# Row sums one group later, tiles scaled by ScalarE, the MLP's first chunk by 256 tokens, and roundings moved, in a two-block transformer kernel

## What is computed

```python
h_x = modulate(x, sh1, sc1)                 # LayerNorm, times 1 + scale, plus shift, from c
mix = (g_f * y_f + g_m * y_m + g_g * y_g) @ w_o      # Fourier, latent and grouped attention, gated
x = layer_norm(alpha * x + g1 * mix, ln1_g, ln1_b)
x = layer_norm(alpha * x + g2 * sq_relu_mlp(modulate(x, sh2, sc2)), ln2_g, ln2_b)
def sq_relu_mlp(h): return square(relu(h @ w1)) @ w2          # 1024 -> 4096 -> 1024
```

## Time and profile before

| what | us |
|---|---|
| three runs, median (lowest, highest) | 3475.98 (3465.0, 3476.44) |
| the profiled execution | 3469.96 |
| its span in the profile | 3468.2 |
| granted PE clock, mean | 0.95 |

### The profile page before, as it was taken

How to read it: one execution, slowest core, us unless ns; L and a number is a source line. 1 busy time by engine, 2 the same in 40 slices (tenths; PEclk the granted TensorE clock), 3 DMA queues, 4 the chain that set the end, 5 groups by cost and what they waited for, 6 DMA issues and landing times.

```text
span 3468.2 us, 37534 instructions
## 1 busy us (share of the span) xinstructions
PE 3159.9 (91%) x15004; PEld 2460.1 (71%) x15004; DVE 2010.8 (58%) x2992; ACT 988.4 (28%) x1725; POOL 950.2 (27%) x702
## 2 busy tenths in 40 slices
PE   6998999999999999979899999699988888888798
PEld 3975666777478888869465665488868766777576
DVE  4566764444655555573576454666665846667354
ACT  3135761000131111131366000322231135421352
POOL 1004766331210000010277663200000425431262
PEclk9999999999999999989899999899999889999799
DMA  6411004343222112123101555132222210113100
GB/s 200 159 47 28 10 28 130 107 110 100 73 73 73 67 56 73 49 89 108 28 1 37 173 161 173 51 113 97 97 78 74 95 49 1 49 61 100 49 1 25
DMA packets 206333, 268.23 MB, mean 77 GB/s; under 512 B 29280, under 2 KB 133680, under 8 KB 205648
## 3 DMA queue, kind: packets, MB, share of 16 engines
q1 hardware_dynamic: 204080, 265.83, 23.7%
q10 hardware_dynamic: 2080, 0.01, 0.0%
HBM read 255.17 MB, written 10.52 MB: 77 GB/s over the span
## 4 chain that ended last, share of the span: by engine, by line
PE 37%; DVE 8%; ACT 2%; POOL 2%; issue 2%; DMA 0%; DVEq 0%; ACTq 0%
PE ps L366 14%; PE ps L1868 5%; PE ps L1878 4%; PE ps L2346 2%; PE ps L1320 2%; PE ps L1303 1%; PE ps L2676 1%; PE ps L1273 1%; DVE stat L651 1%; PE ps L2621 1%; PE ps L1683 1%; DVE U L589 1%; PE ps L1085 1%; PE ps L3030 1%; DVE U L2791 1%
## 5 line engine op out<-in xcount | busy, mean ns | idle before, releaser
L744 POOL TENSOR_TENSOR ht_lo<-HT,ht_hi 128x1024 fp32r<-128x1024 f32 x28 | 69.1, 2467 | 1106.5 <-ACT ht_hi L726 731.1
L1868 PE MATMUL ps<-ht_hi,w_hi 128*128 128x512 f32 (+1 forms) x768 | 273.8, 357 | 14.1 <-issue 12.5
L1868 PE MATMUL ps<-ht_lo,w_hi 128*128 128x512 f32 (+1 forms) x768 | 273.0, 355 | 0.0
L1868 PE MATMUL ps<-ht_hi,w_lo 128*128 128x512 f32 (+1 forms) x768 | 272.9, 355 | 0.0
L1878 PE MATMUL ps<-w_hi,a_hi 128*128 128x512 f32 x640 | 252.1, 394 | 4.3 <-DVE a_lo L1985 4.3
L1878 PE MATMUL ps<-w_lo,a_hi 128*128 128x512 f32 x640 | 251.2, 393 | 0.0
L1878 PE MATMUL ps<-w_hi,a_lo 128*128 128x512 f32 x640 | 250.9, 392 | 0.0
L366 PE MATMUL ps<-w_lo,ht_hi 128*128 128x320 f32 (+2 forms) x800 | 245.2, 307 | 0.0
L1487 POOL TENSOR_TENSOR p_lo<-ring,p_hi 128x512 fp32r<-128x512 f32 x156 | 200.1, 1293 | 117.0 <-DVE p_hi L1442 88.6
L366 PE MATMUL ps<-gate_ht_hi,gate_w_hi 128*128 128x512 f32 (+1 forms) x576 | 224.0, 389 | 1.6 <-POOL w_lo L397 1.6
L366 PE MATMUL ps<-U,ring 128*128 128x512 f32 (+1 forms) x576 | 217.9, 521 | 0.0
(11 more groups left out here) (414 smaller groups left out, 8084.2 us busy)
## 6 DMA issues: line engine op xcount, KB each, us to landing
ring<-w_dram SPq DMA_DIRECT2D x30, 2048.0 KB, 8.1
U<-w_ada_dram SPq DMA_DIRECT2D x80, 512.0 KB, 3.6
ring<-w_in_dram SPq DMA_DIRECT2D x48, 512.0 KB, 6.2
ring<-w_in_dram SPq DMA_DIRECT2D x8, 1280.0 KB, 5.7
ring<-a_w_in_dram SPq DMA_DIRECT2D x8, 1280.0 KB, 6.7
ring<-w_ada_dram SPq DMA_DIRECT2D x4, 2048.0 KB, 10.8
hi_scratch<-ht_hi SPq DMA_DIRECT2D x2, 3072.0 KB, 10.7
gate_ht_hi<-hi_scratch SPq DMA_DIRECT2D x8, 768.0 KB, 4.4
```

The source lines that it names most:

```text
L744: pool.tensor_tensor(HT_LO[:, :, tokens], HT[:, :, tokens], HT_HI[:, :, tokens].bitcast(F32), ALU.subtract).then_inc(ht_ready.sem, 1)
L1868: last = pe.matmul(ps[:, g % 4, 0:c1 - c0], lhsT, rhs, start=(k + j == 0), stop=(k == KD - 1 and j == 2))
```

## The change

Five things. **(1)** In `gemm` with G = 3, a slot's row sums are reduced by PE at group 2 instead of group 1, and the last slot's PE and DVE steps go into `mix_norm`. **(2)** In `mix_norm`, layer 1 does both halves of tile 0 first. The normed tile is written by ACT, from RSTD and a one-element shift by DVE; ACT's order is placing of t-2, roots, scaling of t, and in tile 1 the rounding of W1 behind it. **(3)** Chunk 0 of the MLP goes by 256 tokens: twelve groups in layer 0, eight in layer 1. Its first groups need only tiles 0 and 1. Tiles 4 and 5 (layer 0, at groups 3 and 6) or 2 and 3 (layer 1, at groups 2 and 4) are turned and placed within it, and the rounding of W1's next chunk moves to group 7 or 5. **(4)** In `normed_heads`, slot 0's weights are rounded by ACT ahead, POOL only subtracts. **(5)** In the entry of the last layer, ACT rounds the weights before it places tiles, high and low parts 6 and 7 are one operation each instead of two, tile 4's norm comes before the second slot, and the queries' root stands one group earlier.

```diff
@@ -349,7 +349,7 @@
     between(pe, (i * 2 + s) * G + g)
-if macs and g == 1:
+if macs and g == (2 if G == 3 else 1):
@@ -389,10 +389,9 @@
 if name[s] == "vector":
-    rounding = eng.tensor_copy(h, w)
-else:
-    rounding = eng.tensor_tensor(h, w, one, ALU.mult)
-rounding.then_inc(w_rounded[s].sem, 1)
+    eng.tensor_copy(h, w).then_inc(w_rounded[s].sem, 1)
+elif name[s] == "gpsimd":
+    eng.tensor_tensor(h, w, one, ALU.mult).then_inc(w_rounded[s].sem, 1)
@@ -1637,8 +1636,6 @@
 gemm(G, mms, evac, 3, (("gpsimd", "gpsimd"), 24 * P, GATE_W, 6), False, ready, loads, macs)
-macs.pe(nc.tensor, KD - 1)
-macs.take(nc.vector, KD - 1)
@@ -1647,20 +1644,27 @@
 TIMES = ALPHA * ALPHA
-def wo_bank(t):
-    return 4 + 2 * (1 - t % 2)
-def mix_xn(t):
-    return XN if t < 4 else view(at_att + 4096 + t % 2 * D + D, D)
-def mix_turn_bank(t):
-    return 2 * (t % 2) if t < 4 else wo_bank(t)
+def wo_bank(l, t):
+    return 4 + 2 * (t % 2 if l else 1 - t % 2)
+def mix_xn(l, t):
+    return XN if t < 3 - l else view(at_att + 4096 + t % 2 * D + D, D)
+def mix_late(l):
+    return {2: 2, 4: 3} if l else {3: 4, 6: 5}
+def mix_turn_bank(l, t):
+    return wo_bank(l, t) if t in mix_late(l).values() else 2 * (t % 2)
 def mix_norm(l, nq, G, macs):
-    order = [(0, 0), (1, 0), (0, 1), (1, 1)] + [(t, h) for t in range(2, nq) for h in range(2)]
+    order = ([(0, 0), (0, 1), (1, 0), (1, 1)] if l else [(0, 0), (1, 0), (0, 1), (1, 1)]) + [(t, h) for t in range(2, nq) for h in range(2)]
     place = {th: i for i, th in enumerate(order)}
+    second = place[0, 1]
+    late = mix_late(l).values()
@@ -1673,21 +1677,20 @@
         pe.wait_ge(mixed.sem, mixed_now)
+    if i == second:
+        pe.wait_ge(wo_loaded.sem, wo_loaded.n + 16)
     if i == 2:
+        macs.pe(pe, KD - 1)
         macs.all_taken(pe)
-        pe.wait_ge(wo_loaded.sem, wo_loaded.n + 16)
...
-        last = pe.matmul(ps[:, wo_bank(t) + h, :], MIX[:, k, t * P:(t + 1) * P], w[:, k, :],
+        last = pe.matmul(ps[:, wo_bank(l, t) + h, :], MIX[:, k, t * P:(t + 1) * P], w[:, k, :],
...
-        turn_tile(pe, p, t - 2, mix_xn(t - 2), mix_turn_bank(t - 2))
-if nq == XT:
-    for t in range(nq - 2, nq):
-        turn_tile(pe, p, t, mix_xn(t), mix_turn_bank(t))
+        turn_tile(pe, p, t - 2, mix_xn(l, t - 2), mix_turn_bank(l, t - 2))
@@ -1709,16 +1712,21 @@
     spread(dve, p, t, TIMES * EPS, 2 * t + 1)
-    if 0 < t < 4:
-        dve.wait_ge(turn_done.sem, p.turned + t)
-    dve.tensor_scalar(mix_xn(t), X[:, t, :], MV[:, t, 0:1], RSTD[:, t:t + 1],
-                      ALU.subtract, ALU.mult).then_inc(xn_ready.sem, 1)
+    dve.tensor_scalar(SHIFT[:, t:t + 1], MV[:, t, 0:1], RSTD[:, t:t + 1], -1.0, ALU.mult,
+                      ALU.mult).then_inc(scales_ready.sem, 1)
...
-residual(1, 0)
-norms(0, residual(0, 1))
+if l == 0:
+    residual(1, 0)
+    macs.take(dve, KD - 1)
+    norms(0, residual(0, 1))
+else:
+    i = residual(0, 1)
+    macs.take(dve, KD - 1)
+    norms(0, i)
+    residual(1, 0)
@@ -1726,18 +1734,21 @@
 def _(act):
-    macs.all_taken(act)
     for t in range(nq):
+        if t == 2:
+            macs.all_taken(act)
         if t >= 2:
-            place_tile(act, p, l, 3, t - 2, mix_turn_bank(t - 2))
+            place_tile(act, p, l, 3, t - 2, mix_turn_bank(l, t - 2))
...
+        act.wait_ge(scales_ready.sem, scales_ready.n + t + 1)
+        if t in ((1,) if l else (1, 2, 5)):
+            act.wait_ge(turn_done.sem, p.turned + (4 if t == 5 else t))
+        act.activation(mix_xn(l, t), X[:, t, :], ACT.Identity, scale=RSTD[:, t:t + 1],
+                       bias=SHIFT[:, t:t + 1]).then_inc(xn_ready.sem, 1)
...
-    if nq == XT:
-        for t in range(nq - 2, nq):
-            place_tile(act, p, l, 3, t, mix_turn_bank(t))
@@ -1745,13 +1756,14 @@
         for t in range(nq):
-            if t < 4:
+            if t not in late:
...
+scales_ready.n += nq
@@ -1793,14 +1805,26 @@
 nh = len(halves)
+first_halves = [(c, c + 256) for c in range(0, nq * P, 256)]
 G, Z = CH * nh, 2 * nq
+def halves_of(c):
+    return halves if c else first_halves
+def groups(c):
+    return CH * len(halves_of(c))
+def at(c, g=0):
+    return g + sum(groups(i) for i in range(c))
...
-late = range(4, nq)
+late = mix_late(l)
@@ -1853,14 +1877,17 @@
 pe.wait_ge(split[w].sem, split[w].n + c)
-for g in range(G):
-    f, (c0, c1) = g % CH, halves[g // CH]
+for g in range(groups(c)):
+    f, (c0, c1) = g % CH, halves_of(c)[g // CH]
+    if c == 0 and g in late:
+        turn_tile(pe, mix, late[g], mix_xn(l, late[g]), mix_turn_bank(l, late[g]))
     if c == 0 and g % CH == 0:
-        pe.wait_ge(ht_ready.sem, mix.ht + (4 if g == 0 else nq))
-    if c == 0 and g in (1, 2) and g - 1 < len(late):
-        turn_tile(pe, mix, late[g - 1], mix_xn(late[g - 1]), mix_turn_bank(late[g - 1]))
-    pe.wait_ge(h_taken.sem, h_taken.n + c * G + g - 3)
+        pe.wait_ge(ht_ready.sem, mix.ht + c1 // P)
+    if c == 0 and g in (0, 2):
+        pe.wait_ge(turn_taken.sem, mix.taken + nq - 3 + g // 2)
+    if at(c, g) >= 3:
+        pe.wait_ge(h_taken.sem, h_taken.n + at(c, g) - 3)
@@ -1914,13 +1941,15 @@
         turn_tile(pe, p, first + t, xn, 2 * (t % 2))
+placed_at = {2: 2, 3: 3} if l else late
...
-        c0, c1 = halves[g // CH]
-        act.wait_ge(h_ready.sem, h_ready.n + c * G + g + 1)
-        act.wait_ge(a_ready.sem, a_ready.n + c * G + g - 1)
+        c0, c1 = halves_of(c)[g // CH]
+        act.wait_ge(h_ready.sem, h_ready.n + at(c, g) + 1)
+        act.wait_ge(a_ready.sem, a_ready.n + at(c, g) - 1)
@@ -1936,15 +1965,16 @@
         root(act, p, t, n)
-for g in range(G):
-    if g == next_w2:
+for g in range(groups(c)):
+    if c == 0 and g in placed_at:
+        t = placed_at[g]
+        place_tile(act, mix, l, 3, t, mix_turn_bank(l, t))
+    if g == (next_w2 if c else max(late) + 1):
...
-    if c == 0 and g in (1, 2) and g - 1 < len(late):
-        place_tile(act, mix, l, 3, late[g - 1], mix_turn_bank(late[g - 1]))
@@ -2389,7 +2420,9 @@
             entry.norm(dve, t)
-if not entry:
+if entry:
+    entry.norm(dve, XT)
+else:
@@ -2429,8 +2462,7 @@
 act.activation(first[1], four[1][:, 0:2, :], ACT.Copy)
-for k in (6, 7):
-    act.activation(B_HI[k][:, tokens], four[1][:, k - 4, :], ACT.Copy)
+act.activation(B_LAST[:, :, tokens], four[1][:, 2:4, :], ACT.Copy)
@@ -2447,8 +2479,7 @@
 pool.tensor_tensor(lo[:, 4:6], x[:, 4:6], B_NEXT[:, :, tokens].bitcast(F32), ALU.subtract)
-for k in (6, 7):
-    last = pool.tensor_tensor(lo[:, k], x[:, k], B_HI[k][:, tokens].bitcast(F32), ALU.subtract)
+last = pool.tensor_tensor(lo[:, 6:8], x[:, 6:8], B_LAST[:, :, tokens].bitcast(F32), ALU.subtract)
@@ -3216,7 +3247,7 @@
 def beside(act, g):
-    if g == 2:
+    if g == 1:
@@ -3240,23 +3271,22 @@
     if slot_index == 1:
-        for t in range(XT, NT):
-            entry.norm(dve, t)
+        entry.norm(dve, XT + 1)
 def beside(act, slot_index, g):
-    if slot_index == 1 and g >= 2:
-        root(act, entry.p, g + 2, g + 2)
     if slot_index == 1 and g == 3:
+        root(act, entry.p, XT + 1, XT + 1)
...
-        for t in range(XT):
+        root(act, entry.p, 0, 0)
+        entry.weights_rounded(act, 0)
+        for t in range(1, XT):
+            entry.weights_rounded(act, t)
             root(act, entry.p, t, t)
-            if t:
-                entry.weights_rounded(act, t - 1)
-                entry.place(act, t - 1)
-        entry.weights_rounded(act, XT - 1)
+            entry.place(act, t - 1)
+        root(act, entry.p, XT, XT)
@@ -3330,7 +3360,16 @@
         norms.root(act)
-features(tiles, src, dst, ACT.Silu, w_hi, "gpsimd", beside, join=False)
+with block(False) as b:
+    @b.scalar
+    def _(act):
+        act.wait_ge(ring_full[0].sem, ring_full[0].n + 16)
+        for q in range(4):
+            piece = slice(q * tiles * 2 * P, (q + 1) * tiles * 2 * P)
+            act.activation(w_hi[0][:, piece], ring[0][:, piece], ACT.Copy).then_inc(w_rounded[0].sem, 1)
+features(tiles, src, dst, ACT.Silu, w_hi, ("rest", "gpsimd"), beside, join=False)
```

More of the change, by code:

```diff
@@ L1833, in _ @@
                             second_loads(sp)
-                        sp.wait_ge(h_ready.sem, h_ready.n + c * G)
+                        sp.wait_ge(h_ready.sem, h_ready.n + at(c))
                         if c > 1:
@@ L1880, in products, with output @@
                         return last
-                    def output(z, at, chunks):
-                        pe.wait_ge(z_taken.sem, z_taken.n + at + z - 3)
+                    def output(z, base, chunks):
+                        pe.wait_ge(z_taken.sem, z_taken.n + base + z - 3)
                         for i, (c, s) in enumerate(chunks):
@@ L1978, in hidden @@
                     def hidden(c, g):
-                        f, (c0, c1) = g % CH, halves[g // CH]
+                        f, (c0, c1) = g % CH, halves_of(c)[g // CH]
                         r = RELU[:, g % 2, 0:c1 - c0]
                         hi, lo = A_HI[c % 2][:, f, c0:c1], A_LO[c % 2][:, f, c0:c1]
```

(19 more changed lines are left out.)

8 lines of the change are left out of this document (4 added, 4 removed).

## The result

The changed kernel took 3439.07 us (median of 4 runs, 3436.93 to 3445.21), the kernel before in the same comparison 3471.55 (4 runs, 3465.0 to 3476.44). The ratio is 0.9911, 95% interval 0.9886 to 0.9935: -30.9 us, -22.6 to -39.6. Two further comparisons of the same two kernels gave 0.9923 (0.9904 to 0.9942) and 0.9927 (0.9911 to 0.9943), -26.7 and -25.3 us. Faster by over 0.5% had 0.48, and the change is faster by 0.7 to 0.9% in the three comparisons.

The account below looks back on a forecast made before the run. TensorE, busy for 91% of the span, was taken as the bound, with gains only where it idles or its clock is low. Terms -1.2+4-1-9.5-7.5-3.6 = -18.8 us took the 3475.98 median to 3457, range 3446 to 3471.

Parts of the forecast that it names:

- Part A: Layer 1's gated slots: row sums a group later save 0.3 us in some four slots, -1.2 us, bounds 0 and -2.
- Part B, layer 0: Layer 0's norms and first MLP chunk: tiles take 13.76 us for 11.78, chunk 1 starts later, +4 us, bounds -7 and +8.
- the relu's wait: Layer 0's chunk 0: ScalarE scales tile 5 before its first relu, so TensorE waits some 4.6 us for it.
- The rival with shorter tiles: Norms: a tile takes 11.18 us, layer 0 gives -7 instead of +4, sum -30, 3446 us; chance 0.14.
- Layer 1: Layer 1's norms and first MLP chunk: chunk 1 at 2250.2 to 2251 against 2251.9, -1 us, bounds -4 and +2.
- about 5 us earlier: Layer 1's norms: VectorE starts tile 0 about 5 us earlier, but gains only 1.2 us of it for tile 1.
- Head features: First slot of the head features: ScalarE rounds, GpSimd subtracts, first result at 2754.3 to 2755.7 against 2763.86, -9.5 us.
- Entry: Last layer's entry: tile 0's rest earlier, -4 to -5.5 us, and tile 4's turning without its 2.30 us wait; -7.5 us.
- what ends the wait next is VectorE's splitting: Entry: TensorE's wait is next ended by VectorE's splitting of the weights, which ends beside it; no cost given.
- Root: Q6 of the queries: ScalarE's root one group earlier, ahead of two copies, -3.6 us, bounds 0 and -4.
- The slow rival: Chunk 0's 20 half groups at the low clock, 2.89 us more each; 14 more give 3498 us; chance 0.06.
- It doesn't do what it says: Early rounding, weights first and earlier root buy nothing because the weights' landing binds them; +2 us, 3478; chance 0.05.

Follow-up runs that it names:

- the third trace: The changed kernel profiled and run a third time, nothing further altered, compared with the kernel before: 3444.93 us, ratio 0.9927.
- the control: The kernel before, unchanged, run again under a label of its own against the kernel before: 3464.23 us, ratio 0.9993 (0.998 to 1.0007).

## Why the prediction was right or wrong

**Part A** was -1.2 us in the gates: -0.5 to -1.6, where the kernels with the gates as before show -0.9 to +1.0. Right within what can be read.

**Part B, layer 0**, +4: +3.4 to +4.9. Right, and by its own steps: 13.7 us a tile, the relu's wait, the late chunk 1. Two smaller errors cancel in it. The first relu comes at 978.86, which is 985.5 on the scale of the trace before and not 988.3. Against that, after the wait of 4.43 us TensorE's next 28 matmuls start 0.21 us apart instead of 0.12 (granted clock 0.55 from 979 to 986), 2.6 us where the sum had 1.4, and then it waits 0.8 to 1.9 us for tile 5's rest, which the sum did not hold. The rival with shorter tiles was wrong for this kernel and is what the run with VectorE's scaling shows: the period falls to 11.8 us and layer 0 to -3.0 (its -7 needed 11.18).

**Layer 1**, -1 with bounds -4 and +2: -4.3 to -5.4. The first step that failed is the one that let tile 0 start "about 5 us earlier" and tile 1 "only 1.2, since the take and the locks above lie between". In the traces tile 0 starts 11 us earlier (22.7 for 33.9) and tile 1 6 us (38.3 for 44.4). The row sums' 5.3 us stood ahead of all of W_o, and the row sums alone bring tile 1 5.2 us forward. I charged the take and the lock of GpSimd's subtraction of W1 against it, which the kernel before pays as well: VectorE's L694 takes 8.56 us in tile 2 in both. Behind tile 1 the forecast's 2.2 us for the rounding of W1 is there (2.3), one of the two longer tiles (1.9), and the "some 3 later" for ScalarE's placing of tile 1 is not. In the third trace tile 3 is scaled by 2212.0, which is 2218.8 on the scale of the trace before, where the forecast had 2229. Of these 10 us only 4.4 arrive, since TensorE turns tile 3 ahead of group 4, at 2219.1, 7 us after it is scaled. (In the trace before tile 3's scaling is over at 2219.9, not at 2220.6.) Undone order and changed order give the same.

**Head features**, -9.5: -9.5 in all three. Right. The first result is at 2745.41, which is 2754.6 on the scale of the trace before, for 2754.3 to 2755.7. The second slot's pieces were not late.

**Entry**, -7.5 from terms of -4 to -5.5 and 2.3: -10.4 us. Tile 0's rest starts at 3033.9 on the scale of the trace before, as forecast, and the first product at 3037.0, 5.6 us earlier; tile 4's turning no longer waits its 2.3. The other 2.5 us were in no term; the granted clock of the entry is 0.94 (3001 to 3063) where it was 0.88 (3015 to 3088). But "what ends the wait next is VectorE's splitting" was named and costed at nothing: behind the entry the traces show 3.6 to 7.5 us more. Not all of it is the change's, since the control has the same wait of 2.8 us and +3.4 in that stretch, and the clock there is 0.96 in the third trace and 1.00 in the first. Means over all traces without and with the changed entry differ by -10.3 in the entry and +3.7 behind it: -6.6 together, so -7.5 was near by two errors that cancel. The part alone gave -11.4 (-6.6 to -16.3).

**Root**, -3.6: -3.1. Right.

**The sum** was -18.8, the stages show -17.5 to -20.8: too little gain in layer 1 and the entry, and too little cost behind the entry, cancel each other. The runs say -25 to -31, and the time fell below the range. Two more steps failed there. The first is the base, "and put it to the latter": the median of three runs, 3475.98. The kernel before has 3471.55 in the same comparison, 3469.15 over 35 runs and 3464 to 3470 in the others, so 4 to 7 us of the 18 from 3457 to 3439 were in the base. That alone does not mend it: from 3471.55 the range would have been 3442 to 3467, and from 3469.15 it would have been 3439.2 to 3464.2, just above the 3439.07 measured. The second is the range. It was made of the terms alone, as if unchanged stretches took the same time in every run; they differ by up to 11.6 us in the traces. The rival with shorter tiles had -30 us and the first comparison gave -30.9, but its tiles of 11.18 us did not come: that number agrees by luck.

**What stays open** is the distance between the stages' sum and the ratios of three comparisons, -25 to -31. Against the mean of all traces without the change, instead of the first one alone, the stages' sum is near -21 (+4.9, -0.9, -5.4, -9.6, -10.3, +3.7, -3.1), and -22 with the stretch from 1027 to 1799. That lies inside the intervals of the two later comparisons (-20 to -33 and -20 to -31) and just outside the first one's (-22.6 to -39.6). The mean of two traces of the kernel before and that of three of the changed one lie 22.3 us apart at 3400 us. It may be that the clock lapses less often in the changed kernel; no run separates that from chance. The slow rival, chunk 0 at the low clock, did not occur: 0.93 in that window. "It doesn't do what it says" did not either, as the waits that went show.

## What to carry to other kernels

Before moving an operation off a busy engine, look up what then meets what: here 0.60 us a tile saved on VectorE moved GpSimd's 2.4 us onto it, and taking the move back gave 13 us. The same meeting, of one GpSimd operation with one of VectorE, made the wait behind the entry, by the traces. A wait ahead of a whole stage is worth most of its length to everything in the stage (here 4.0 of 5.3 us), and what the kernel pays already is not to be charged to the change again. Take the base of a forecast from many runs, and put the wander of unchanged stretches into its range.

## What the runs showed of the hardware that was not expected

VectorE's one-column operation with two inputs takes 0.22 us free and 2.11 us when a GpSimd subtraction of 128x1024 has started 0.24 us ahead of it. A rounding of 128x1024 costs GpSimd 2.06 us where ScalarE does four in 3.88, and GpSimd's four subtractions then take 11.39 us, 1.2 more than four of the earlier trace rows would, without moving the first result away from its forecast place. The first of them takes 3.45 us: it starts at 2732.27, while VectorE's two-input L2319 runs from 2730.16 to 2733.52. VectorE's rounding copy of 128x768 takes 0.56 us free and 2.60 when a GpSimd subtraction has started 0.26 us ahead of it. The granted clock of the same 20 us of unchanged attention was 0.66, 0.76 and 0.92 in three traces; no cause for it was found.
